# Eight orders of columns inside the matmuls of a two-layer hybrid backbone (one Trainium2 core)

## The reference, cut to what matters

```python
def swiglu(z, w_in, w_out):
    gate, up = jnp.split(z @ w_in, 2, axis=-1)
    return (jax.nn.silu(gate) * up) @ w_out

h = h + 0.5 * m[2] * swiglu(modulate(rmsnorm(h, ffn1_norm_g[l]), m[0], m[1]),
                            ffn1_w_in[l], ffn1_w_out[l])
```

## Time and profile before

| | us |
|---|---|
| median of 2 runs | 1577.57 |
| lowest, highest | 1577.11, 1578.04 |
| span of the profiled execution | 1575.5 |
| median less span (what lies around it) | 2.1 |
| PE busy | 1561.2 |
| DVE busy | 1001.6 |
| ACT busy | 631.0 |

### The profile page before, as it was taken

The page is one execution under the profiler, slowest core; times in us unless marked ns, Lnnn a source line. Parts: engine busy times, 40 slices in busy tenths (PEclk is TensorE's granted clock), DMA queues, the critical chain, the costliest instruction groups (busy, mean ns, idle before and its releaser), DMA issues.

```text
span 1575.5 us, 22302 instructions
## 1 busy us (share of the span) xinstructions
PE 1561.2 (99%) x9052; PEld 1338.1 (85%) x9052; DVE 1001.6 (64%) x1243; ACT 631.0 (40%) x856; POOL 82.5 (5%) x100
## 2 busy tenths in 40 slices
PE   8999999999999999999999999999999999999998
PEld 6888888888988888888888898888888897999998
DVE  5776773783967577777364267777445358975554
ACT  4433322332784343323222243333232249764553
POOL 0000000011100200000000100000000111000001
PEclk9999999999999999999999999999999999999999
DMA  9565553653322355565353336556354323456563
GB/s 365 201 197 179 186 162 119 208 192 94 115 75 79 94 166 193 176 201 173 107 196 99 107 121 201 193 183 195 100 173 148 107 91 108 147 188 197 190 203 117
DMA packets 71786, 249.95 MB, mean 159 GB/s; under 512 B 11664, under 2 KB 11920, under 8 KB 70672
## 3 DMA queue, kind: packets, MB, share of 16 engines
q1 hardware_dynamic: 71696, 248.70, 48.1%
HBM read 247.62 MB, written 1.05 MB: 158 GB/s over the span
## 4 chain that ended last, share of the span: by engine, by line
PE 96%; DVE 2%; ACT 1%; issue 0%; POOL 0%; POOLq 0%; DVEq 0%; ACTq 0%
PE bank L437 85%; PE bank L574 2%; PE bank L580 2%; PE bank L576 2%; PE bank L452 1%; PE bank L475 1%; PE bank L747 1%; PE bank L720 1%; PE bank L718 1%; PE bank L719 1%; PE bank L749 0%; PE bank L468 0%; DVE w_lo L1174 0%; PE bank L529 0%; PE bank L460 0%
## 5 line engine op out<-in xcount | busy, mean ns | idle before, releaser
L877 ACT ACTIVATE w_hi<-raw 128x1024 fp32r<-128x1024 f32 x317 | 335.9, 1060 | 807.0 <-PE bank L437 792.8
L1174 DVE TENSOR_TENSOR w_lo<-raw,w_hi 128x1024 fp32r<-128x1024 f32 x317 | 387.7, 1225 | 371.9 <-ACT w_hi L877 371.6
L437 PE MATMUL bank<-z_hi,w_hi 128*128 128x512 f32 (+1 forms) x1480 | 535.9, 362 | 2.4 <-DVE w_lo L1174 1.9
L437 PE MATMUL bank<-z_lo,w_hi 128*128 128x512 f32 (+1 forms) x1480 | 532.1, 360 | 0.0
L437 PE MATMUL bank<-z_hi,w_lo 128*128 128x512 f32 (+1 forms) x1480 | 531.9, 359 | 0.0
L437 PEld LDWEIGHTS bank<-z_hi,w_hi 128*128 128x128 f32 x1480 | 278.0, 188 | 49.7 <-DVE w_lo L1174 3.2
L437 PEld LDWEIGHTS bank<-z_hi,w_lo 128*128 128x128 f32 x1480 | 278.0, 188 | 42.6
L437 PEld LDWEIGHTS bank<-z_lo,w_hi 128*128 128x128 f32 x1480 | 278.1, 188 | 42.6 <-issue 1.0
L437 PE MATMUL bank<-h_hi,w_hi 128*128 128x512 f32 (+1 forms) x770 | 266.5, 346 | 0.0
L437 PE MATMUL bank<-h_lo,w_hi 128*128 128x512 f32 (+1 forms) x770 | 265.7, 345 | 0.0
L437 PE MATMUL bank<-h_hi,w_lo 128*128 128x512 f32 (+1 forms) x770 | 265.6, 345 | 0.0
(11 more groups left out here) (185 smaller groups left out, 1234.3 us busy)
## 6 DMA issues: line engine op xcount, KB each, us to landing
raw<-weights SPq DMA_DIRECT2D x320, 512.0 KB, 4.1
ada_raw<-ada_w SPq DMA_DIRECT2D x128, 512.0 KB, 4.2
ada_head<-head_w SPq DMA_DIRECT2D x8, 1024.0 KB, 18.5
res<-x_t SPq DMA_DIRECT2D x4, 512.0 KB, 4.8
ada_raw<-gate_w SPq DMA_DIRECT2D x4, 256.0 KB, 5.3
ws<-sgu_w SPq DMA_DIRECT2D x2, 256.0 KB, 4.0
bs<-sgu_b SPq DMA_DIRECT2D x2, 256.0 KB, 4.2
out<-final SPq DMA_DIRECT2D x2, 256.0 KB, 3.0
```

What stands on the lines that cost most here:

```text
L437: m = pe.matmul(bank[:, to], w, x[:, k, at], start=start and i == 0, stop=stop and i == 2, skip_group_check=True)
L877: act.activation(w_hi[:, r, :], raw[:, r, :], ACT.Copy).then_inc(hi_ready, 1)
L1174: dve.tensor_tensor(w_lo[:, r, :], raw[:, r, :], w_hi[:, r, :].bitcast(F32), ALU.subtract).then_inc(lo_ready, 1)
```

## The change

A function `in_order(row, order)` returns the same columns of a row in another order, by a rearranged access pattern. `product` gets a parameter `order` and applies it to the bank and to the moving operand alike. `slot` passes `(i * 4 + p) % 8` in the written-out up projections, `row` passes `(dd + 1) % 8` with two streams. All other products keep order 0. With lines of 16 columns, numbered 0 to 31: order 1 is all even lines, then all odd; 2 all odd, then all even; 3 the second half of the columns, then the first; 4 lines 0, 16, 1, 17 and on; 5 each two neighbours swapped; 6 as order 4 with pieces of 32 columns; 7 as order 1 with pieces of 8 columns.

```diff
+ORDERS = 8
...
+            def in_order(row, order):
+
+                if order == 1:
+                    return row.rearrange("p (l h i) -> p h l i", h=2, i=16)
+                if order == 2:
+                    return row.rearrange("p (l h i) -> p h l i", h=2, i=16)[:, ::-1]
+                if order == 3:
+                    return row.rearrange("p (h i) -> p h i", h=2)[:, ::-1]
+                if order == 4:
+                    return row.rearrange("p (h l i) -> p l h i", h=2, i=16)
+                if order == 5:
+                    return row.rearrange("p (l h i) -> p h l i", h=2, i=16)[:, :, ::-1]
+                if order == 6:
+                    return row.rearrange("p (h l i) -> p l h i", h=2, i=32)
+                if order == 7:
+                    return row.rearrange("p (l h i) -> p h l i", h=2, i=8)
+                return row
...
-                    m = pe.matmul(bank[:, to], w, x[:, k, at], start=start and i == 0,
+                    m = pe.matmul(in_order(bank[:, to], order), w, in_order(x[:, k, at], order), start=start and i == 0,
                                   stop=stop and i == 2, skip_group_check=True)
...
+                    order = (i * 4 + p) % ORDERS if at["mods"] else 0
                     for k in range(KD):
-                        m = product(pa[q], k, q, z_hi, z_lo, k, part, k == 0, k == KD - 1)
+                        m = product(pa[q], k, q, z_hi, z_lo, k, part, k == 0, k == KD - 1, order=order)
...
-                            m = product(po[dd % 2], b, q % RING, h_hi, h_lo, k, all_of(len(ss)), k == 0, k == KF - 1)
+                            m = product(po[dd % 2], b, q % RING, h_hi, h_lo, k, all_of(len(ss)), k == 0, k == KF - 1,
+                                        order=(dd + 1) % ORDERS if len(ss) == 2 else 0)
```

More of the change, by code:

```diff
@@ L430, in _, with product @@
         def _(pe):
-            def product(bank, blk, r, x_hi, x_lo, k, part, start, stop, ahead=None):
+            def in_order(row, order):
[8 more added lines that the diff above has]
+                if order == 5:
+                    return row.rearrange("p (l h i) -> p l h i", h=2, i=16)[:, :, ::-1]
+                if order == 6:
[3 more added lines that the diff above has]
+                return row
+            def product(bank, blk, r, x_hi, x_lo, k, part, start, stop, ahead=None, order=0):
                 c = slice(blk * P, (blk + 1) * P)
```

## The result

The changed kernel takes 1613.17 us against 1577.57, a ratio of 1.0224 with a 95% interval of 1.0207 to 1.024. The forecast was 1573.6 with a range up to 1612.0: the kernel became slower where a slight gain was forecast, and the range is missed by 1.2 us. The span of the profiled execution went from 1575.5 to 1611.0 us, by 35.5.

A forecast was written before the change was run, and what follows sets the result against it. TensorE's 226.7 ns product step was taken as the bound; span 1575.5 - 4 for fewer collisions = 1571.5, plus about 2.1 us around the span, gave 1573.6 us, with 8 in 10 between 1548 and 1612.

The forecast's parts named there:

- What bounds the kernel: TensorE's step of 226.7 ns per 512-column product bounds these stages; a change of it reaches the end undiluted.
- The count: Changed products: 2592 in up projections and 1386 in down rows, together 3978, so each nanosecond per product is 3.98 us.
- the term of -1 ns a product: Changed products: seven orders spread around the old loss, most at 32 cycles, some at 16; average about -1 ns, -4 us.
- The two rows behind the term: 256-column products: 113.5 ns read from column 112, losing 16 cycles; 120 ns read from column 0, losing 32.
- (a): Rival on the moving read: the loss is the same in any order, 226.7 ns throughout, 1577.6 us; chance 0.25.
- The theory of the loss: In each product the moving read collides with the neighbouring weight load in a memory bank; address order decides how often.
- signs of a wrong mechanism: In the changed products: steps varying inside one order, or differing between up and down for the same order.
- (b): Rival on changed products: orders break most collisions, -6.7 to -10 ns each, 1551 to 1538 us; chance 0.13.
- (c): Rival on read or bank side: each jump costs a cycle at full rate, 47 us, 1625 us; chance 0.20.
- the eight free jumps: Modulation sums reading 8 runs of 32 columns at half rate: eight jumps for under 2 ns, counted against jump costs.
- the upper bound from the earlier trace: Changed products: the worst steady step, about 240 ns, in all orders would add 13 ns each, +52 us.

The follow-up runs named there:

- e1: Changed kernel with the eight orders on the moving operand alone, the bank written straight; 1616.88 us, ratio 1.0234 to the kernel before.
- e3: Straight reads instead of orders, weight block or moving operand read 0 to 112 columns later; weights alone: 226.8 ns a product at 64 columns, 233 at 8 and 16.
- e11: Straight reads instead of orders; weights and tokens shifted together: 227 to 229 ns a product; weights alone at seven new shifts: 233 to 234 ns.
- e4: Changed kernel with other orders on source and bank: runs of 4 to 128 columns, or lines backwards; 226.7 ns a product (runs of 128) to 250 (runs of 4).
- e9: Changed kernel reading lines of 16 columns, each s lines after the last, bank straight; s = 5 and 9: 227 ns a product, s = 4 and 8: 242.5.
- e5: Changed kernel with order 4 in all written-out up slots, order 6 in two-stream down rows, weights shifted 0 to 56 columns; order 4 240 ns at every shift.
- e6: Changed kernel loading 128, 96, 64 or 32 weight columns in two up projections, straight or order 4, order 0 elsewhere; order 4 240 ns at every width.
- e8: Straight reads, layer 1's first up projection altered by index: 1 every second 2-byte element, 225.0 ns; 2 each column twice, 215.8; 3 each line twice, 240.
- e10: Changed kernel with all seven orders made of runs of 64 or more columns, right result; 1577.53 us against 1577.74 before, ratio 0.9995.
- e2: Changed kernel with the eight orders on the bank alone, the moving operand read straight; 1578.17 us, ratio 0.9999 to the kernel before.

## Why the prediction was wrong

**What bounds the kernel** held: TensorE's step is what counts, it goes to the end undiluted, nothing else moved. The count held too: with the steps in excess of 226.7 ns from the slots of e1 and the timeline, for orders 1, 2, 4, 5, 6, 7 and 0, then for order 3, 360 x (13.3 + 10.3 + 13.3 + 9.8 + 9.9 + 6.3 + 1.1) + 432 x 1.2 ns = 23.6 us in up slots (1.1 is what a slot in order 0 pays, mostly on entering from order 7), and 198 x (13.3 + 10.1 + 0.4 + 13.3 + 9.9 + 9.9 + 5.7) = 12.4 us in down rows (orders 1 to 7). Together 36.0, measured 35.5, of which the earlier start gives back 0.2.

**The step that failed** is "the order from column 0 upwards isn't special as to collisions; it already pays 32 cycles where another start pays 16". From 113.5 against 120 ns at 256 columns I concluded that the sequence was one draw among many, and that seven others would scatter around it. In the sum this is the term of -1 ns a product, -4 us; measured are +9 ns a product, +35.6 us, a mean step near 235.6 ns where the prediction allowed 222 to 231. The runs show why: of the fifteen relative places in e3 and e11 and of the orders in e1, e4 and e9, none was under 226.7 ns. A straight read at the present place sits at the bottom, and one can leave it only upwards. The two rows behind the term don't carry it. They differ in more than the start column (other loops, other weights), the loop of 113.5 ns runs at 117.8 in other traces (last section), which is a loss of 27 cycles instead of 16 at the same start, and at 512 columns e3 has nothing that gains at such a place. The equal step of z and h products in the earlier trace rows, listed for rival (a), may mean only that both stand at the same good place: the down rows of e3 give the same curve as its up slots (233 at 8 columns, 229 at 112).

**The theory of the loss** was half right. Right: it is on the read side, and for straight reads the neighbouring weight load's place matters (e3, e11). Wrong: that this collision decides what the orders cost. e5 and e6 leave order 4 at 240 ns whatever the weights do; e8 shows that at half the rate of lines the loss is 6 cycles with the weight load still there. The prediction's own signs of a wrong mechanism stayed away: steps are constant inside an order, and up and down agree for each within 1 ns (order 2 237.1 and 236.8, order 5 236.2 and 236.7). They couldn't tell a collision with the weights from a loss of the moving read by itself.

**The rivals.** (a), no change, needed a loss that no order alters. (b) never appeared. (c) had the right side and was 12 us off (1625), but by a mechanism that e9 refutes: 31 jumps at s = 5 cost nothing and 7 jumps in e10 neither, order 6 pays 9.9 ns for 15 jumps and order 7 6.3 for 63. Its other half, the bank's side, costs nothing (e2). Its support against, the eight free jumps of the earlier trace rows, may have been free for another reason: those runs are 32 columns long but read at half rate, where e8's index 2 loses 6 cycles only. Orders in plain fp32 were not run. I gave (c) 0.20 and cut the range inside it; as no row showed a full-rate read in short runs, the upper bound from the earlier trace rows, 240 ns for all, 52 us, was the honest end, and the average came to two thirds of it.

**Open.** Why lines out of turn cost 1.8 to 2.2 cycles each where those in turn cost 1, why runs of 4 and 8 cost less than 16 when even and odd runs are read one after the other, and what fixes the straight loss at 32 cycles, isn't settled. Memory banks of 64 bytes, four in turn, are the simplest picture that gives the period in e3 and e9; it wasn't shown directly, and it doesn't say why order 1 takes 240 ns and order 2, the same two halves the other way round, 237.

## What to carry to other kernels

In these fp32r matmuls of 512 columns, where TensorE was the bound, the order of the moving read had a price. Token permutations in runs of 64 columns or more (256 bytes, starting at a multiple of that), or with 16-column line following line in a turn of four, were free; runs of 4 to 32 cost 2 to 10% of every product (231 to 250 ns against 226.7). PSUM writes in pieces of 8, 16, 32 and 256 fp32 values cost nothing, so put a needed permutation on the output. Before taking "another order may collide less" as a draw from a hat, look whether the layout of before is already at the bottom: change one address in a probe and see on which side it falls.

## What was not expected

The period of four lines (e9), and a straight read that depends on the address of the weights (e3: 5.46 us a slot against 5.60), stood in none of the prediction's cases.

Nor was this: the 1512 products of the last two loops, the same code in all kernels, run at one of two steps. The chain's piece for them is 171.47 us in the kernel after (shown above); in e1 it is:

```profile
1430.88 178.16 PE bank L453 x1512
```

That is 113.4 or 117.8 ns a product, 6.7 us in all. Of the thirteen traces e1, e8 and e11 have the longer piece (178.16, 178.17 and 178.27 us), the other ten 171.46 to 171.60, and nothing lies between. A possible reading is that the two reads lock into one of two phases at the loop's start; it wasn't tested.
